# The prompt's attention gates as tanh inside the attention: ScalarE and VectorE in place of sigmoids and Pool's products in the first sample

## The chip, the cores and the metric

The kernel runs on one core of one Trainium2 chip. The metric is device time in microseconds of one launch of the whole kernel; lower is better. All arithmetic is float32.

## The reference, cut to what matters

One decoder layer with two branches. A prompt of 512 tokens and 8 samples of 8 tokens each share one input projection. The attention branch of 16 heads (8 pairs of heads, 64 values each) is multiplied by a SiLU gate of the projected column block `z_a`:

```python
o_a = _prompt_attention(q, keys, vals) * jax.nn.silu(z_a)            # prompt: 512 tokens
o_a_s = _sample_attention(q_s, kv_s, ...) * jax.nn.silu(z_a_s)       # samples: 8 x 8 tokens, 4096 past keys each
# silu(z) = z * sigmoid(z) = 0.5 * z * (1 + tanh(z / 2))
```

The rest of the layer (a low-rank query and key path, an RWKV-7 branch, a gated merge, an output projection) is not touched by the change.

## The kernel before, in words

Each engine has a program of its own; stages follow each other without a barrier, and only semaphores order the engines. The stages are `front` (projection of the latent columns, queries, keys, values), `prompt` (the prompt's attention), `absorb` (a short bridge that folds the key up-projection into the samples' queries), `sample` (8 samples of 4096 keys, each in 8 groups of 512 keys), `rwkv` and `merge`.

`prompt` runs over 8 pairs of heads and, in a pair, over 8 units u (4 blocks of 128 queries, 2 heads), 64 units in all. Unit w of a pair sees (w//2 + 1) x 128 keys. Written out by hand, the order is this:
- TensorE, at step u: scores of unit u+2 (`score`, L727); a few of the 128 matmuls that make the gate columns of `hT` (`gates`, L739), 16 halves e of 288 columns with 8 matmuls each, into two PSUM banks `psZ`; the values of the last two units (`values`, L758) when u is even; at the first step of a pair the spread of the former pair's inverse sums (L771); the transposes of unit u (L748). `values` and `transposes` wait for the copies of the units before (`tr_sb`).
- VectorE, at step u: `top(u)`, the mask, the row maximum and its product (L809, L811, L813). At w = 0, 1, 2 of the next pair also the inverse sums (L819, L823) and `output` (L828, L830): psB is copied to `oaT` and multiplied by the values in `psO`.
- ScalarE, at step u: the exponentials of unit u+2 (L855), which wait for `top(u+2)`, then the copy of unit u's transposes to `pT` (L862), which `values` and the next transposes wait for, then the finished gate half e from `psZ` to `zraw` (`gates_to_sbuf`, L866; the semaphore `z_sb` frees the bank).

So at w = 2 of a pair, VectorE does `top(u)`, then `output` of the former pair, then `top(u+1)`; ScalarE's exponentials of u+1 wait for that, and its copy to `pT` stands behind them.

After the prompt VectorE copies the key weights (L962) and the queries (L967), TensorE makes the absorbed queries (L905), and these go through DRAM to the samples.

`sample` begins with group 0 of sample 0. Per group TensorE makes scores (L1141, L1145) and turns the former group's (L1152); ScalarE copies scores out of PSUM (L1235); VectorE transposes the latents of the group after next (L1285), weights the turned scores (L1321) and keeps a running maximum (L1325, both inputs in SBUF). In sample 0 nothing is yet to be multiplied with the latents, so a group is short. In its first seven groups ScalarE also computes the sigmoid of `zraw`, one pair at a time (`gate_sigmoid`, L912), into the spare tile `sgz`, and GpSimd (Pool) multiplies: `zraw` by the sigmoid (L917), a copy of the sample columns to `zas` (L920), `oaT` by the gate (L921). When all 8 pairs are done (`gated`), the queue of SyncE stores `oaT` to DRAM, and VectorE may weight the first group of sample 1. Much later `gate_samples` (L1387) multiplies the samples' attention by `zas`.

Of the kernel before, what the change touches and what calls it, by code (L numbers as in the profile page):

```python
# [15 lines left out]
KT = D // P  # L16
# [606 lines left out]
def prompt(nc, I, M):  # L623

    with ExitStack() as ctx:
# [11 lines left out]
        M.sgz = pT[:, :, :].rearrange("p a t -> p (a t)")[:, 4 * SEQ - 2 * USED:4 * SEQ].rearrange("p (a t) -> p a t", a=2)  # L637
# [9 lines left out]
        scores, maxed, exped, tr, tr_sb, pv, z_mm, z_sb, inv, inv_tr, inv_sb, spread, o_sb = (  # L647
            sem(n) for n in ("scores", "maxed", "exped", "tr", "tr_sb", "pv", "z_mm", "z_sb", "inv", "inv_tr", "inv_sb", "spread", "o_sb"))
# [4 lines left out]
        M.exped, M.tr_sb, M.zraw_sb, M.pv, M.o_sb = exped, tr_sb, z_sb, pv, o_sb  # L653
# [145 lines left out]
        @block.vector  # L799
        def _(dve):  # L800
            v = nc.vector
            dve.drain()
            dve.wait_ge(fixed_in, 32)

            def top(u):
                hp, qb, nk, c = u // NU, u % NU // 2, cols(u), u % 8
                h = 2 * hp + u % 2
                dve.wait_ge(scores, u + 1)
                v.tensor_tensor(psS[u % 3][:, qb * P:nk], psS[u % 3][:, qb * P:nk], tri[:, :], ALU.add)  # L809
                dve.drain()  # L810
                v.tensor_reduce(mx[:, c:c + 1], psS[u % 3][:, 0:nk], AX.X, ALU.max)  # L811
                dve.drain()
                v.scalar_tensor_tensor(nmx[:, c:c + 1], mx[:, c:c + 1], -1.0, M.qs[:, qb, h:h + 1], ALU.mult, ALU.mult).then_inc(maxed, 1)  # L813

            def inverses(hp):
                dve.wait_ge(exped, NU * (hp + 1))
                if hp > 0:
                    dve.wait_ge(inv_tr, hp)
                v.reciprocal(ri[:, :], rs[:, hp % 2, :]).then_inc(inv, 1)  # L819

            def inverses_to_sbuf(hp):
                dve.wait_ge(inv_tr, hp + 1)
                v.tensor_copy(riT[:, :], psB[0:8, 0:P]).then_inc(inv_sb, 1)  # L823

            def output(hp):
                dve.wait_ge(spread, hp + 1)
                dve.wait_ge(pv, PB * (hp + 1))
                v.tensor_copy(M.oaT[:, hp, 0:SEQ], psB[:, :])  # L828
                dve.drain()
                v.tensor_tensor(M.oaT[:, hp, 0:SEQ], psO[:, :], M.oaT[:, hp, 0:SEQ], ALU.mult).then_inc(o_sb, 1)  # L830

            for u in range(ALL + 3):
                if u < ALL:
                    top(u)
                hp, w = u // NU, u % NU
                if hp > 0:
                    if w == 0:
                        inverses(hp - 1)
                    if w == 1:
                        inverses_to_sbuf(hp - 1)  # L840
                    if w == 2:
                        output(hp - 1)

        @block.scalar
        def _(act):
# [18 lines left out]
            def gates_to_sbuf(e):  # L864
                act.wait_ge(z_mm, e + 1)
                nc.scalar.copy(M.zraw[:, e // 2, e % 2 * HT:(e % 2 + 1) * HT], psZ[e % 2][:, 0:HT]).then_inc(z_sb, 1)  # L866
# [6 lines left out]
            gates_to_sbuf(0)  # L873
            gates_to_sbuf(1)
            for u in range(ALL):
# [3 lines left out]
                for e in range(begun[u] // KT, begun[u + 1] // KT):  # L879
                    gates_to_sbuf(e)  # L880
            for e in range(begun[ALL] // KT, 2 * NP):
                gates_to_sbuf(e)

def absorb(nc, I, M):

    with ExitStack() as ctx:
# [3 lines left out]
        qgT, sg = M.spare[:, 0:NP * SB].rearrange("p (h t) -> p h t", t=SB), M.sgz  # L891
        bank = [ctx.enter_context(nc.psum_tensor(f"ab_bank{i}", [P, 512], F32)) for i in range(8)]
        half_bank, product_banks = (bank[7], bank[5]), ((bank[2], bank[3]), (bank[4], bank[6]))
        tr, tr_sb, mm, ev, act_sb, sigmoids, silus, gated = (sem(n) for n in ("tr", "tr_sb", "mm", "ev", "act_sb", "sigmoids", "silus", "gated"))
# [14 lines left out]
        def gate_sigmoid(act, hp):  # L909
            if hp >= 2:  # L910
                act.wait_ge(silus, hp - 1)
            nc.scalar.activation(sg[:, hp % 2, :], M.zraw[:, hp, :], ACT.Sigmoid).then_inc(sigmoids, 1)  # L912

        def gate(pool, hp):
            v = nc.gpsimd
            pool.wait_ge(sigmoids, hp + 1)
            v.tensor_tensor(M.zraw[:, hp, :], M.zraw[:, hp, :], sg[:, hp % 2, :], ALU.mult).then_inc(silus, 1)  # L917
            pool.wait_ge(M.o_sb, hp + 1)
            pool.drain()
            v.tensor_copy(M.zas[:, hp, :], M.zraw[:, hp, SEQ:USED])  # L920
            v.tensor_tensor(M.oaT[:, hp, 0:SEQ], M.oaT[:, hp, 0:SEQ], M.zraw[:, hp, 0:SEQ], ALU.mult).then_inc(gated, 1)  # L921

        M.absorb_products, M.gate_sigmoid, M.gate_prompt = products, gate_sigmoid, gate
        M.absorb_tr, M.uk_sb, M.absorb_ev, M.gated = tr, uk_sb, ev, gated

# [83 lines left out]
def sample(nc, I, M):  # L1009

    with ExitStack() as ctx:
# [46 lines left out]
        def _(pool):  # L1058
            for hp in range(NP):
                M.gate_prompt(pool, hp)  # L1060
# [167 lines left out]
        def _(act):  # L1228
# [30 lines left out]
            M.gate_sigmoid(act, 0)  # L1259
            M.gate_sigmoid(act, 1)  # L1260
            for i in range(ALL):
                n, g = i // G, i % G
                scores_to_sbuf(i)
                if n == 0 and g > 0 and g + 1 < NP:
                    M.gate_sigmoid(act, g + 1)
# [10 lines left out]
        def _(dve):  # L1276
# [1931 lines left out]
```

## Time and profile before

| | |
|---|---|
| median of 3 runs | 1582.36 us (1582.04 to 1584.71) |
| the profiled execution | 1585.03 us, of which the span from first to last instruction is 1583.2 us |
| prompt's attention, first scores that are waited for to last output | about 186 to 341 us |
| first sample | about 357 to 386 us |
| mean granted TensorE clock | 0.996 |
| TensorE busy, share of the span | 1522.3 us, 96% |
| VectorE, ScalarE, Pool busy | 822.8, 548.6 and 248.8 us |

A row of the timeline has the start and the duration in us, the engine, the line, the operation, output and inputs with their shapes, how many instructions were merged into the row, and in square brackets the idle time of the engine ahead of it and what ended it. PE is TensorE's matmul, PEld its weight load, DVE VectorE, ACT ScalarE, POOL GpSimd. The ends of matmuls are modelled. A matmul of float32 stands in the rows as two instructions.

### The profile page before, as it was taken

The page shows a single profiled execution, that of the slowest core. Times are in us where ns is not written, and L with a number is a line of the kernel's source. Part 1 is how long each engine was busy: PE and PEld are TensorE (multiplying, and loading weights), DVE is VectorE, ACT ScalarE, POOL GpSimd, SP SyncE. Part 2 cuts the span into 40 slices and gives each one's busy share as a digit, 9 for nine tenths or more (in the row PEclk, how much of TensorE's full clock was granted, in tenths as well). Part 3 has the DMA queues.
Part 4 walks back from the last instruction along what each step waited for, and adds up shares of the span by engine and source line. Part 5 has one row for each costly group of instructions (what it writes and reads, how often), then busy time and mean ns, then how long its engine had stood idle before and what let it go on. Part 6 is the DMA issues. An engine that isn't in the chain of part 4 may idle for free.

```text
span 1583.2 us, 40939 instructions
## 1 busy us (share of the span) xinstructions
PE 1522.3 (96%) x16954; PEld 1113.1 (70%) x16954; DVE 822.8 (52%) x1664; ACT 548.6 (35%) x1339; POOL 248.8 (16%) x303
## 2 busy tenths in 40 slices
PE   6999999988999999998999999999999999999998
PEld 4455566657888888776777767677767677777753
DVE  3153445457877777555656565656666522113422
ACT  3056444432222222244353535353535232210000
POOL 0000130235111111110000000000000045446200
PEclk9999999999999999999999999999999999999999
DMA  9713687723455565420112112111111125342302
GB/s 332 275 53 107 204 222 273 197 73 111 126 146 147 144 152 148 112 54 19 35 41 47 50 35 52 30 50 31 49 29 49 33 51 180 80 159 81 113 10 76
DMA packets 192100, 165.30 MB, mean 104 GB/s; under 512 B 38586, under 2 KB 170938, under 8 KB 190892
## 3 DMA queue, kind: packets, MB, share of 16 engines
q1 hardware_dynamic: 182636, 127.13, 28.5%
q0 software_dynamic: 8352, 32.52, 6.7%
q8 instruction: 134, 2.20, 0.6%
q10 hardware_dynamic: 928, 3.05, 0.6%
q14 instruction: 50, 0.41, 0.1%
HBM read 136.97 MB, written 25.69 MB: 103 GB/s over the span
## 4 chain that ended last, share of the span: by engine, by line
PE 65%; DVE 6%; ACT 5%; DVEq 2%; issue 2%; DMA 0%; SPq 0%; POOL 0%; ACTq 0%
PE me_bank L2902 12%; PE rw_bank L1715 10%; PE sa_psOs L1182 7%; PE sa_psS L1145 7%; PE me_bank L2922 3%; PE rw_bank L1754 2%; PE sa_psT L1152 2%; DVE rw_gram L2479 2%; PE sa_psS L1141 2%; PE rw_bank L1816 2%; PE rw_bank L1835 1%; PE rw_bank L1727 1%; PE rw_bank L1740 1%; PE rw_bank L1967 1%; PE rw_bank L1887 1%
## 5 line engine op out<-in xcount | busy, mean ns | idle before, releaser
L1715 PE MATMUL rw_bank<-hT,big 128*128 128x288 f32 x672 | 183.6, 418 | 0.0
L1715 PEld LDWEIGHTS rw_bank<-hT,big 128*128 128x128 f32 x672 | 122.4, 190 | 32.4 <-issue 1.2
L1235 ACT COPY kpe<-sa_psS 128x512 f32<-128x512 f32 x64 | 37.5, 586 | 211.4 <-PE sa_psS L1145 211.4
L1513 POOL COPY shc<-prep 128x3 f32<-128x3 f32 x8 | 1.5, 190 | 473.0 <-ACT rw_xs L2181 473.0
L1740 PE MATMUL rw_bank<-hT,big 128*128 128x288 f32 x256 | 73.5, 421 | 0.0
L739 PE MATMUL pr_psZ<-hT,qlT 128*128 128x288 f32 x256 | 73.1, 406 | 0.1
L1321 DVE TENSOR_TENSOR sa_ST<-sa_psT,kinvp 128x512 f32<-128x512 f32 x64 | 43.8, 685 | 50.2 <-PE sa_psT L1152 47.2
L2961 ACT COPY big<-me_bank 128x288 f32<-128x288 f32 x42 | 16.8, 399 | 144.8 <-PE me_bank L2902 144.8
L855 ACT ACTIVATE pr_pb<-pr_psS,pr_nmx,qs 128x128 f32<-128x128 f32 (+3 forms) x64 | 39.5, 618 | 77.3 <-PE pr_psT L748 46.3
L1145 PE MATMUL sa_psS<-sa_cT_blocks,qg 32*128 32x128 f32 x2048 | 64.6, 274 | 0.0
L1145 PE MATMUL sa_psS<-sa_cT_blocks,qlT 32*128 32x128 f32 x2048 | 63.0, 270 | 0.0
L2499 DVE COPY_PREDICATED rw_X<-lev,rw_bank 128x128 f32<-128x128 int32 (+1 forms) x80 | 20.9, 261 | 79.6 <-PE rw_bank L1835 79.6
L1182 PE MATMUL sa_psOs<-big,sa_ST 128*128 128x257 f32 x256 | 61.1, 381 | 1.2 <-ACT sa_ol_raw L1251 1.2
L1182 PE MATMUL sa_psOs<-pages,sa_ST 128*128 128x257 f32 x256 | 61.0, 381 | 1.2 <-ACT sa_ol_raw L1251 1.2
L1145 PEld LDWEIGHTS sa_psS<-sa_cT_blocks,qg 32*128 32x128 f32 x2048 | 61.9, 191 | 0.0
L739 PEld LDWEIGHTS pr_psZ<-hT,qlT 128*128 128x128 f32 x256 | 46.9, 189 | 20.7 <-issue 9.0
L1145 PEld LDWEIGHTS sa_psS<-sa_cT_blocks,qlT 32*128 32x128 f32 x2048 | 60.3, 187 | 0.0
L1740 PEld LDWEIGHTS rw_bank<-hT,big 128*128 128x128 f32 x256 | 44.9, 189 | 20.1 <-issue 11.5
L994 POOL DMA_DIRECT2D pages<-in_cache_kv x68 | 37.6, 553 | 126.8 <-issue 126.8
L994 POOL DMA_DIRECT2D big<-in_cache_kv x68 | 37.6, 554 | 118.4 <-issue 118.4
L2902 PE MATMUL me_bank<-prep,me_arena 128*128 128x288 f32 x208 | 53.4, 406 | 0.0
L1182 PEld LDWEIGHTS sa_psOs<-pages,sa_ST 128*128 128x128 f32 x256 | 46.5, 190 | 8.2 <-ACT sa_ol_raw L1251 1.9
(547 smaller groups left out, 3346.4 us busy)
## 6 DMA issues: line engine op xcount, KB each, us to landing
big<-in_w_in SPq DMA_DIRECT2D x44, 512.0 KB, 4.0
big<-in_cache_kv POOLq DMA_DIRECT2D x68, 128.0 KB, 3.2
pages<-in_cache_kv POOLq DMA_DIRECT2D x68, 128.0 KB, 2.8
fr_wada<-in_w_ada SPq DMA_DIRECT2D x8, 1024.0 KB, 11.4
big<-in_cache_kv SPq DMA_DIRECT2D x60, 128.0 KB, 2.9
pages<-in_cache_kv SPq DMA_DIRECT2D x60, 128.0 KB, 3.0
qk_scratch<-oaT SPq DMA_DIRECT2D x32, 192.0 KB, 2.5
fr_wada<-in_w_ada SPq DMA_DIRECT2D x2, 2048.0 KB, 10.4
```

The lines of the kernel that those rows point to most:

```text
L739: last = nc.tensor.matmul(psZ[h][:, 0:HT], M.wz[hp % 2][:, k, :], M.hT[:, k, h * HT:(h + 1) * HT], start=(k == 0), stop=(k == KT - 1))
L855: nc.scalar.activation(pb[:, u % 2, 0:cols(u)], psS[u % 3][:, 0:cols(u)], ACT.Exp, bias=nmx[:, c:c + 1], scale=M.qs[:, qb, h:h + 1], accum ...
L994: e.dma_start(M.pages[s % 2][q * QP:(q + 1) * QP, g, :, 0:KL], src).then_inc(landed, 16)
L1141: nc.tensor.matmul(psS[:, b, 0:ROW], M.qpT[rows, n, :, :].rearrange("p h t -> p (h t)"), kT[rows, g, :], start=True, stop=False)
L1145: done = nc.tensor.matmul(psS[:, b, 0:ROW], q4[n % 2][rows, a, :], cT[rows, g % 2, a, :], start=False, stop=(a == NCB - 1))
L1182: done = nc.tensor.matmul(psO[:, 0:C1], STs[s % 2][:, GP * g + c, :], M.pages[s % 2][:, g, c, :], start=(g == 0 and c == 0), stop=False)
L1235: nc.scalar.copy(S[:, i % 2, :].rearrange("q (c p j) -> q p c j", c=GP, p=GP), got).then_inc(copied, 1)
L1321: v.tensor_tensor(group, psT[i % 2][:, :].rearrange("p (a h t) -> p a h t", h=H, t=TD), bc(ki, TD, 3), ALU.mult).then_inc(weighted, 1)
L1715: last = mm(bank[h][:, 0:HT], w[:, ORDER[q], k, :], M.hT[:, k, (F0, F1)[h]], start=(k == 0), stop=(k == KT - 1))
L1740: last = mm(bank[h][:, 0:HT], w[:, 3, k, :], M.hT[:, k, (F0, F1)[h]], start=(k == 0), stop=(k == KT - 1))
L2902: last = nc.tensor.matmul(into[:, 0:HT], st[:, k, :], mv[:, k, :], start=(k == 0 and n in (1, 2, 7)), stop=(k == KT // 2 - 1), skip_group_ ...
L2922: last = nc.tensor.matmul(out_bank[o][:, :], mT[k][:, b * P:(b + 1) * P], wo[k][:, n * 512:(n + 1) * 512], start=(k == 0), stop=(k == KT - 1))
```

## The change

ScalarE reads each finished gate half from PSUM through `Tanh` with scale 0.5, in place of the plain copy. VectorE then computes (tanh + 1) * z from `zraw` and the PSUM bank, which is twice the SiLU; only then is the bank free. `output` of a pair gets a third operation: `oaT` = (gate * 0.5) * `oaT`. The sample columns go straight to `zas`, and `gate_samples` multiplies by 0.5 as well. The sigmoids on ScalarE and everything of Pool's in the first sample are removed, with the spare tile and VectorE's wait for `gated` at sample 1.

VectorE takes the halves three steps after TensorE finished them, behind `top(u)`; halves 0 and 1 behind `top(1)`. Worked out from the tables `in_pair`, half e is taken at u = 6, 10, 14, 19, 24, 28, 33, 37, 42, 46, 51, 56, 62, 66 for e = 2 to 15, which is w = 6, 2, 6, 3, 0, 4, 1, 5, 2, 6, 3, 0, 6, 2.

```diff
+                dve.drain()
+                v.scalar_tensor_tensor(M.oaT[:, hp, 0:SEQ], M.zraw[:, hp, 0:SEQ], 0.5, M.oaT[:, hp, 0:SEQ], ALU.mult, ALU.mult).then_inc(gated, 1)
+            def twice_silu(e):
+                hp = e // 2
+                dve.wait_ge(z_tanh, e + 1)
+                if e % 2 == 0:
+                    half = M.zraw[:, hp, 0:HT]
+                    v.scalar_tensor_tensor(half, half, 1.0, psZ[0][:, 0:HT], ALU.add, ALU.mult).then_inc(z_sb, 1)
+                else:
+                    half = M.zraw[:, hp, HT:SEQ]
+                    v.scalar_tensor_tensor(half, half, 1.0, psZ[1][:, 0:SEQ - HT], ALU.add, ALU.mult)
+                    v.scalar_tensor_tensor(M.zas[:, hp, :], M.zraw[:, hp, SEQ:USED], 1.0, psZ[1][:, SEQ - HT:HT], ALU.add, ALU.mult).then_inc(z_sb, 1)
             for u in range(ALL + 3):
                 if u < ALL:
                     top(u)
+                if u == 1:
+                    twice_silu(0)
+                    twice_silu(1)
+                if u >= 3:
+                    for e in range(begun[u - 3] // KT, begun[u - 2] // KT if u - 2 < ALL else 2 * NP):
+                        twice_silu(e)
...
-                nc.scalar.copy(M.zraw[:, e // 2, e % 2 * HT:(e % 2 + 1) * HT], psZ[e % 2][:, 0:HT]).then_inc(z_sb, 1)
+                nc.scalar.activation(M.zraw[:, e // 2, e % 2 * HT:(e % 2 + 1) * HT], psZ[e % 2][:, 0:HT], ACT.Tanh, scale=0.5).then_inc(z_tanh, 1)
...
-        def gate_sigmoid(act, hp):
-            if hp >= 2:
-                act.wait_ge(silus, hp - 1)
-            nc.scalar.activation(sg[:, hp % 2, :], M.zraw[:, hp, :], ACT.Sigmoid).then_inc(sigmoids, 1)
-        def gate(pool, hp):
-            v = nc.gpsimd
-            pool.wait_ge(sigmoids, hp + 1)
-            v.tensor_tensor(M.zraw[:, hp, :], M.zraw[:, hp, :], sg[:, hp % 2, :], ALU.mult).then_inc(silus, 1)
-            pool.wait_ge(M.o_sb, hp + 1)
-            pool.drain()
-            v.tensor_copy(M.zas[:, hp, :], M.zraw[:, hp, SEQ:USED])
-            v.tensor_tensor(M.oaT[:, hp, 0:SEQ], M.oaT[:, hp, 0:SEQ], M.zraw[:, hp, 0:SEQ], ALU.mult).then_inc(gated, 1)
...
-            for hp in range(NP):
-                M.gate_prompt(pool, hp)
...
-                        dve.wait_ge(M.gated, NP)
...
-                v.tensor_tensor(M.zas[:, :, :], o, M.zas[:, :, :], ALU.mult).then_inc(gated, 1)
+                v.scalar_tensor_tensor(M.zas[:, :, :], M.zas[:, :, :], 0.5, o, ALU.mult, ALU.mult).then_inc(gated, 1)
```

## Rows read from the trace of the kernel before

**Rows 1.** Windows, 150 us of prompt, 24 of first sample: busy us (instructions).

```profile
195.00:345.00 150.00, 143.25 (x937) 99.56 (x935) 72.67 (x214) 71.65 (x199) 41.24 (x72) 1.00 0.71 206
362.00:386.00 24.00, 20.57 (x545) 18.17 (x549) 19.94 (x20) 7.60 (x13) 18.46 (x18) 1.00 0.11 30
```

**Rows 2.** Waits, 180 to 345 us: us in total, times, longest.

```profile
PE pr_psO L758 <- ACT pr_pT L862: 5.3, 9, 0.7
```

**Rows 3.** Timeline at `output` of the first pair (w = 2 of the second).

```profile
208.58 0.69 DVE L828 COPY oaT<-pr_psB 128x512 f32<-128x512 f32 x1 [2.05 <-PE pr_psB L771]
...
209.35 0.69 DVE L830 TENSOR_TENSOR oaT<-pr_psO,oaT 128x512 f32<-128x512 f32 x1
...
210.80 1.14 PE L739 MATMUL pr_psZ<-hT,qlT 128*128 128x288 f32 x4
...
211.01 0.56 ACT L855 ACTIVATE pr_pb<-pr_psS,pr_nmx,qs 128x256 f32<-128x256 f32 x1 [1.30 <-DVE pr_nmx L813]
...
211.57 0.25 ACT L862 COPY pr_pT<-pr_psT 128x128 f32<-128x128 f32 x1
...
211.87 0.44 PE L758 MATMUL pr_psO<-pr_pT,pr_vh 128*64 128x128 f32 x4
```

**Rows 4.** Timeline in the last pair, behind `output` of the seventh.

```profile
325.03 0.44 PE L758 MATMUL pr_psO<-pr_pT,pr_vh 128*64 128x128 f32 x4 [0.58 <-ACT pr_pT L862]
```

**Rows 5.** Timeline at the start of the prompt's attention.

```profile
186.71 0.30 DVE L809 TENSOR_TENSOR pr_psS<-pr_psS,pr_tri 128x128 f32<-128x128 f32 x1
...
188.10 0.69 ACT L866 COPY pr_zraw<-pr_psZ 128x288 f32<-128x288 f32 x2
...
188.67 0.59 ACT L855 ACTIVATE pr_pb<-pr_psS,pr_nmx,qs 128x256 f32<-128x256 f32 x1
...
189.23 0.28 ACT L862 COPY pr_pT<-pr_psT 128x128 f32<-128x128 f32 x1
...
190.17 0.27 PE L748 MATMUL pr_psT<-ident_sb,pr_pb 128*128 128x128 f32 x1
```

**Rows 6.** Timeline behind the last `output`.

```profile
341.09 1.22 DVE L962 COPY pr_wuk<-ab_bank 128x512 f32<-128x512 f32 x2
...
343.49 3.79 PE L905 MATMUL ab_bank<-pr_pb,pr_wuk 64*128 64x64 f32 x64 [0.38 <-DVE pr_pb L967]
```

**Rows 7.** Groups of VectorE by shape: busy us, mean ns, idle before.

```profile
L3011 DVE TENSOR_TENSOR me_arena<-me_bank,big 128x288 f32<-128x288 f32 x16 | 7.3, 458 | 68.8 <-ACT big L2961 35.2 <-PE me_bank L2902 33.6
...
L2531 DVE TENSOR_TENSOR rw_ZRm<-rw_bank,rw_ZR 128x64 f32<-128x64 f32 x8 | 1.7, 214 | 0.0
```

**Rows 8.** Timeline of the first sample, groups 2 to 4, and group 8.

```profile
365.13 0.50 PE L1141 MATMUL sa_psS<-sa_kpeT_blocks,qpT 32*128 32x128 f32 x8 [0.20 <-ACT kpe L1235]
...
368.21 0.50 PE L1141 MATMUL sa_psS<-sa_kpeT_blocks,qpT 32*128 32x128 f32 x8 [0.20 <-ACT kpe L1235]
...
368.73 1.40 POOL L917 TENSOR_TENSOR pr_zraw<-pr_zraw,pr_pT 128x576 f32<-128x576 f32 x1
368.83 1.85 DVE L1325 TENSOR_TENSOR sa_top<-sa_ST 128x512 f32<-128x512 f32 x1
...
371.89 0.50 PE L1141 MATMUL sa_psS<-sa_kpeT_blocks,qpT 32*128 32x128 f32 x8 [0.80 <-DVE sa_cT_blocks L1285]
...
385.57 0.50 PE L1141 MATMUL sa_psS<-sa_kpeT_blocks,qpT 32*128 32x128 f32 x8 [0.21 <-ACT kpe L1235]
```

**Rows 9.** Line L1325 in the whole run: duration in ns, least, median, most.

```profile
L1325 DVE TENSOR_TENSOR sa_top<-sa_top,sa_ST x48: 691/692/1705, 372.5 to 648.5; 128x512 f32<-128x512 f32 x48
```

**Rows 10.** Timeline at the first exponentials of the samples.

```profile
395.61 1.28 ACT L1242 ACT_TABLE_LOAD   x1
...
396.40 1.28 DVE L1344 TENSOR_TENSOR sa_ST<-sa_ST,sa_topB 128x512 f32<-128x512 f32 x2
...
397.12 1.23 ACT L1245 ACTIVATE sa_ST<-sa_ST 128x512 f32<-128x512 f32 x2
```

**Rows 11.** ScalarE's timeline at the tanh behind the samples' last exponentials.

```profile
670.40 0.68 ACT L2320 ACTIVATE big<-big 64x576 f32<-64x576 f32 x1 [3.32 <-DVE big L2606]
```

More of the change, by code:

```diff
@@ L646, in prompt @@
         fixed_in, heads_in = sem("fixed_in"), [sem("heads_in0"), sem("heads_in1")]
-        scores, maxed, exped, tr, tr_sb, pv, z_mm, z_sb, inv, inv_tr, inv_sb, spread, o_sb = (
-            sem(n) for n in ("scores", "maxed", "exped", "tr", "tr_sb", "pv", "z_mm", "z_sb", "inv", "inv_tr", "inv_sb", "spread", "o_sb"))
+        scores, maxed, exped, tr, tr_sb, pv, z_mm, z_tanh, z_sb, inv, inv_tr, inv_sb, spread, o_sb, gated = (
+            sem(n) for n in ("scores", "maxed", "exped", "tr", "tr_sb", "pv", "z_mm", "z_tanh", "z_sb", "inv", "inv_tr", "inv_sb", "spread", "o_sb", "gated"))
         w_v = I["w_in"].rearrange("(k p) n -> p k n", p=P)
@@ L652, in prompt @@
         block = M.block
-        M.exped, M.tr_sb, M.zraw_sb, M.pv, M.o_sb = exped, tr_sb, z_sb, pv, o_sb
+        M.exped, M.tr_sb, M.zraw_sb, M.pv, M.o_sb, M.gated = exped, tr_sb, z_sb, pv, o_sb, gated
         cols = lambda u: (u % NU // 2 + 1) * P
@@ L872, in _ @@
             exponentials(1)
-            gates_to_sbuf(0)
-            gates_to_sbuf(1)
+            gates_tanh(0)
+            gates_tanh(1)
             for u in range(ALL):
@@ L879, in _ @@
                 for e in range(begun[u] // KT, begun[u + 1] // KT):
-                    gates_to_sbuf(e)
+                    gates_tanh(e)
             for e in range(begun[ALL] // KT, 2 * NP):
-                gates_to_sbuf(e)
+                gates_tanh(e)
 def absorb(nc, I, M):
@@ L890, in absorb @@
         ukT = M.wuk[:, :, :]
-        qgT, sg = M.spare[:, 0:NP * SB].rearrange("p (h t) -> p h t", t=SB), M.sgz
+        qgT = M.spare[:, 0:NP * SB].rearrange("p (h t) -> p h t", t=SB)
         bank = [ctx.enter_context(nc.psum_tensor(f"ab_bank{i}", [P, 512], F32)) for i in range(8)]
         half_bank, product_banks = (bank[7], bank[5]), ((bank[2], bank[3]), (bank[4], bank[6]))
-        tr, tr_sb, mm, ev, act_sb, sigmoids, silus, gated = (sem(n) for n in ("tr", "tr_sb", "mm", "ev", "act_sb", "sigmoids", "silus", "gated"))
+        tr, tr_sb, mm, ev, act_sb = (sem(n) for n in ("tr", "tr_sb", "mm", "ev", "act_sb"))
         uk_sb = sem("uk_sb")
@@ L907, in products @@
             last.then_inc(mm, 1)
-        def gate_sigmoid(act, hp):
-            if hp >= 2:
-                act.wait_ge(silus, hp - 1)
-            nc.scalar.activation(sg[:, hp % 2, :], M.zraw[:, hp, :], ACT.Sigmoid).then_inc(sigmoids, 1)
-        def gate(pool, hp):
-            v = nc.gpsimd
-            pool.wait_ge(sigmoids, hp + 1)
-            v.tensor_tensor(M.zraw[:, hp, :], M.zraw[:, hp, :], sg[:, hp % 2, :], ALU.mult).then_inc(silus, 1)
-            pool.wait_ge(M.o_sb, hp + 1)
-            pool.drain()
-            v.tensor_copy(M.zas[:, hp, :], M.zraw[:, hp, SEQ:USED])
-            v.tensor_tensor(M.oaT[:, hp, 0:SEQ], M.oaT[:, hp, 0:SEQ], M.zraw[:, hp, 0:SEQ], ALU.mult).then_inc(gated, 1)
-        M.absorb_products, M.gate_sigmoid, M.gate_prompt = products, gate_sigmoid, gate
-        M.absorb_tr, M.uk_sb, M.absorb_ev, M.gated = tr, uk_sb, ev, gated
+        M.absorb_products, M.absorb_tr, M.uk_sb, M.absorb_ev = products, tr, uk_sb, ev
         @block.tensor
```

7 lines of the change are left out of this document (1 added, 6 removed).

## The prediction

> **What bounds the kernel now.** I read the windows first, because the change moves work between two stages. In 150 us of the prompt [rows 1] TensorE has matmuls for 143.25 us, VectorE and ScalarE for 72.67 and 71.65: the reader is to see a stage that TensorE bounds, with two helpers half idle. That alone would say that new work of VectorE there is free. The waits [rows 2] say the same: TensorE waited for the copies to `pT` for 5.3 us in all. But in a stage where three engines take turns a half idle engine can still be in line at one place. So I read the timeline next, at the places where VectorE gets new work, and followed each step to the matmul behind it. The first sample, the second window of [rows 1], is another case: VectorE is busy for 19.94 of 24 us, Pool for 18.46, TensorE for 20.57, so there TensorE waits 3.4 us in 24.
>
> **ScalarE's tanh for the copy.** 16 reads of 128x288 out of PSUM at 0.35 to 0.4 us (two for 0.69) [rows 5] become 16 activations of the same shape. The nearest activation, with its function read from a table, took 0.59 us for 256 columns with two pointer operands and an accumulator, the copy is shorter; an immediate scale should cost next to nothing, at most 0.1 us each. Hidden: ScalarE is idle half of the time. 
>
> **VectorE's halves.** An operation on 288 columns with one input in PSUM took 0.46 us, on 64 columns 0.21 [rows 7]; for 224 columns I put 0.21 + 160/224 x 0.24 = 0.39. An even half costs 0.46, an odd one 0.39 + 0.21 = 0.60, eight of each 8.5 us. Halves 2 to 15 stand behind `top(u)`, three steps late, when the tanh should be done; the cover is VectorE's wait for the next scores or, at w = 2, its wait of 2.05 us for the spread [rows 3]. I take 0 for these 14. If that cover were gone, all 14 would cost 7 x 0.46 + 7 x 0.60 = 7.4 us. The two at w = 3 (halves 5 and 12) have the thinnest cover, since `output` has just made VectorE late; 0 to 0.5 us each.
>
> **The start.** Halves 0 and 1 are not three steps late. `top(2)` began at 186.71, and now stands behind both halves, which wait for tanh. Those come where the copies are, at 188.10 to 188.79, the first done at about 188.5 [rows 5]. Half 0 then ends at 188.97, half 1 at 189.36 and 189.6. `top(2)` starts at 189.6 and takes about 1.0 (from the end of L830, 210.04, to the exponentials at 211.01 it is 0.97 for the same width [rows 3]), so the exponentials of unit 2 start at 190.6 and not at 188.67. Behind them on ScalarE is the copy of unit 0, which ended at 189.51 and now ends at 191.4, and on TensorE the transposes of unit 1, which came at 190.17 and would come at 191.45: **1.3 us** lost. Bounds: 0.5 (TensorE has more queued than the modelled ends say) and 2.0 (the whole delay of the exponentials).
>
> **The third operation of `output`.** It is 128x512, and L828 to L830, with a drain between, is 209.35 - 208.58 = 0.77 us [rows 3]; the new one adds the same again. What stands behind it? `top(11)`, then ScalarE's exponentials of unit 11, which waited for VectorE (idle 1.30), then on ScalarE the copy of unit 9 (ends 211.82), then the values of TensorE at 211.87. TensorE's gate matmuls ahead of these end at 210.80 + 1.14 = 211.94 [rows 3]. So the chain from VectorE is already in line with TensorE there, with less than 0.1 us to spare. The same rows come behind the outputs of pairs 1 to 6, of which the first is shown. So the copy comes 0.77 late, and TensorE stands for 0.7: 6 x 0.7 = **4.2 us**. In the last pair TensorE has fewer gate matmuls and already stood 0.58 us at this place [rows 4]: **0.77**. Bounds of these seven: from 0.4 each (2.8) to 0.9 each (6.3). Nothing gives it back later, since TensorE's own work then sets the pace.
>
> **Behind the last `output`** VectorE goes on without a gap: L830 to 341.03, the key weights at 341.09, then copies that TensorE waits for until 343.49 [rows 6]. The new operation pushes that whole chain: **0.77 us**. It goes on through the queries to DRAM and back, on which the samples wait, so it isn't hidden. SyncE's queue is not held: its store of `oaT` waits for `gated`, which now comes before it reaches that place, so the 2 MB leave some 20 us earlier, behind the loads of sample 1's queries.
>
> **What the first sample gains.** Pool's products ran together with VectorE's L1325: from 368.83 it took 1.85 us beside L917 [rows 8], where its median in the run is 692 ns [rows 9]. The latents behind it came late and TensorE waited for them (0.80). From group 3 to group 8 it is 385.57 - 368.21 = 17.36 us for five groups, 3.47 each; undisturbed, 368.21 - 365.13 = 3.08 [rows 8]. Five times 3.08 is 15.40, a gain of 1.96; VectorE's transposes of the next keys fall in one of them, so I take **1.9 us**, with bounds of 1.2 and 2.3. The Trainium skill ("SBUF — State Buffer", Who interferes with whom) has the rule: a VectorE instruction with two SBUF inputs and a GpSimd one that reads SBUF exclude each other; the trace agrees with 1.85 against 0.69. By the same rule the new product of `output`, with both inputs in SBUF, could stand behind Pool in the prompt; but there Pool only issues transfers.
>
> **The two table loads.** The sigmoids' load goes, and so does the exponentials' at 395.61, 1.28 us. The exponentials of the scores started at 397.12; VectorE's centring, which they also need, ran from 396.40 for two groups in 1.28, the first done at about 397.05 [rows 10]. So the load is covered: 0, at the most 1.3. The 0.5 in `gate_samples` is a second scalar of one instruction: 0. Pool has nothing else to do in that time: 0.
>
> **The sum.** 1.3 + 4.2 + 0.77 + 0.77 - 1.9 = +5.1 us. The profiled execution took 1585.03 (span 1583.2), so it would be 1590.1; it was itself 2.7 above the median of the runs, to which I add: 1582.36 + 5.1 = 1587.5.
>
> **The rivals.**
> - *The third product is hidden too.* The ends of matmuls are modelled; if TensorE has 0.8 us more queued than the rows say when it reaches the values at w = 2, six pairs cost nothing, and 1.3 + 0.77 + 0.77 - 1.9 = +0.9: 1583.3. For it: only 5.3 us of waits in all [rows 2]. Against it: VectorE's chain ends within 0.1 us of TensorE's [rows 3], and in the last pair TensorE stood [rows 4]. It decides from 0.3 us more slack per pair, which takes 1.8 off the forecast. 0.2.
> - *The first sample pays for all, faster.* The table load at 395.61 is on the path (1.28), Pool's hold is worth its upper bound (2.3), and the prompt hides what it can: 0.9 + 1.9 - 2.3 - 1.28 = -0.8, still no gain above 0.2%. To be faster by that, the start and the last product must be hidden as well: 1582.36 - 2.3 - 1.28 = 1578.8. 0.04.
> - *VectorE's halves are not covered.* A half waits for its tanh in front of the next `top`; from 0.5 us per half on it shows. With the 7.4 us above in full, 1594.9; with a third of it, 1590. 0.14.
> - *Tanh is loaded from another set.* Then each of 16 tanh brings two loads of 1.28 us, as the one of [rows 10], 41 us on ScalarE, of which its idle time of some 1.3 us [rows 3] covers half: some 20 us, 1607. Against it [rows 11]. 0.02.
>
> **How the numbers follow.** The forecast has 0.6. What a measurement of this kernel can tell from no change is about 0.2%, 3.2 us, so slower means above 1585.5 and faster below 1579.2. Slower: 0.6 less a tenth for its lower bounds (0.5 + 2.8 + 0.77 + 0.77 - 2.3 = +2.5), plus 0.14 and 0.02, some 0.70; the hidden product lies within 0.2%; faster 0.04. The range goes from 1582.5, under the first rival, to 1591.0, the forecast with upper bounds for start and products (+0.7 and +1.4) and 1.4 us of uncovered halves; outside it lie the rest of the third rival and the last, and the second.
>
> **What the profile after would show.** L748 of unit 1 some 1.3 us later against the first scores; at w = 2 of each pair a TensorE wait for L862 of about 0.7 us, so that the waits [rows 2] grow from 5.3 to about 11 and each pair gets 0.7 us longer; L905 0.8 later behind the last `output`; in the first sample L1325 at 0.69 throughout and groups of 3.08 us; no load at L1242; no wait of TensorE for `z_sb`. I am wrong if the pairs take the same time as before, or if VectorE waits for tanh in the middle of the prompt.

## The result and the profile after

The changed kernel takes 1593.03 us (median of 4 runs, 1592.73 to 1593.34), the kernel before 1583.17 us in the same comparison (4 runs, 1582.04 to 1584.71): a ratio of 1.0059 [1.0044, 1.0074], 9.9 us slower. The forecast was 1587.5 with a range up to 1591.0, so the direction was right and the size was not.

The profiled execution after took 1593.19 us, its span is 1591.5; before, 1585.03 and 1583.2. Of 9.9 us between the medians the two traces therefore show 8.3.

The waits of TensorE, 180 to 345 us, answer to [rows 2]. They doubled, as forecast (11 us).

```profile
PE pr_psO L757 <- ACT pr_pT L880: 11.1, 15, 1.4
```

The timeline of the changed kernel at the first `output` answers to [rows 3]. L831 is the new operation, and TensorE's values, which came at 211.87 without a wait, now come at 215.25 after 0.73 us of waiting for ScalarE's copy, behind exponentials that waited for VectorE:

```profile
211.17 0.69 DVE L827 COPY oaT<-pr_psB 128x512 f32<-128x512 f32 x1 [1.61 <-PE pr_psB L770]
211.94 0.69 DVE L829 TENSOR_TENSOR oaT<-pr_psO,oaT 128x512 f32<-128x512 f32 x1
212.72 0.69 DVE L831 SCALAR_TENSOR_TENSOR oaT<-pr_zraw,oaT 128x512 f32<-128x512 f32 x1
213.39 1.13 PE L738 MATMUL pr_psZ<-hT,qlT 128*128 128x288 f32 x4
214.39 0.56 ACT L873 ACTIVATE pr_pb<-pr_psS,pr_nmx,qs 128x256 f32<-128x256 f32 x1 [2.09 <-DVE pr_nmx L812]
214.94 0.25 ACT L880 COPY pr_pT<-pr_psT 128x128 f32<-128x128 f32 x1
215.25 0.44 PE L757 MATMUL pr_psO<-pr_pT,pr_vh 128*64 128x128 f32 x4 [0.73 <-ACT pr_pT L880]
```

In the last pair the same place waits 1.38 us; before it was 0.58 [rows 4].

```profile
329.74 0.69 DVE L827 COPY oaT<-pr_psB 128x512 f32<-128x512 f32 x1 [1.78 <-PE pr_psB L770]
333.82 0.44 PE L757 MATMUL pr_psO<-pr_pT,pr_vh 128*64 128x128 f32 x4 [1.38 <-ACT pr_pT L880]
```

The start of the prompt's attention answers to [rows 5]. VectorE stood 1.91 us for the first tanh; the transposes of unit 1 came at 191.82 and not at 190.17. The gate products waited 0.56 us for the bank that half 0 frees, which the forecast had ruled out (no wait of TensorE for `z_sb`):

```profile
186.63 0.60 PE L726 MATMUL pr_psS<-pr_kh,pr_qh 96*128 96x256 f32 x2
188.50 0.70 ACT L884 ACTIVATE pr_zraw<-pr_psZ 128x288 f32<-128x288 f32 x2
188.94 0.46 DVE L838 SCALAR_TENSOR_TENSOR pr_zraw<-pr_zraw,pr_psZ 128x288 f32<-128x288 f32 x1 [1.91 <-ACT pr_zraw L884]
189.54 2.48 PE L738 MATMUL pr_psZ<-hT,qlT 128*128 128x288 f32 x6 [0.56 <-DVE pr_zraw L838]
191.82 0.42 PE L747 MATMUL pr_psT<-ident_sb,pr_pb 128*128 128x128 f32 x1
```

Behind the last `output`, for [rows 6], TensorE stands 1.13 us and not 0.38. The next row is what the forecast did not have: the 64 absorbed products take 6.12 us in place of 3.79.

```profile
353.03 6.12 PE L923 MATMUL ab_bank<-pr_pb,pr_wuk 64*128 64x64 f32 x64 [1.13 <-DVE pr_pb L970]
```

Windows of the changed kernel show why: the column behind POOL is TensorE's granted clock (1.00 is 2.4 GHz, 0.50 is 1.2). About 1 us after that pause it is at half, and it had also fallen at the start, where before it stayed at 1.00.

```profile
190.00:192.00 2.00, 2.00 (x7) 1.19 (x6) 1.41 (x6) 0.81 (x3) 1.74 (x3) 0.57 0.95 234
192.00:194.00 2.00, 2.00 (x7) 1.24 (x5) 0.37 (x2) 0.81 (x3) 1.14 (x3) 0.57 0.99 418
...
352.00:354.00 2.00, 0.97 (x18) 1.00 (x19) 1.97 (x4) 0.00 (x0) 0.00 (x0) 1.00 0.04 8
354.00:356.00 2.00, 2.00 (x25) 2.00 (x23) 0.23 (x1) 0.00 (x0) 0.00 (x0) 0.53 0.00 0
356.00:358.00 2.00, 2.00 (x22) 2.00 (x22) 1.06 (x2) 0.00 (x0) 0.00 (x0) 0.50 0.04 8
```

In the first sample, for [rows 8], TensorE's timeline (starts of L1142) has groups of 3.07 to 3.08 us (372.19 to 375.26, 378.34, 381.41), and L1321, line L1325 of before [rows 9], takes 694 ns at most. The gain is there. But one group takes 5.67 us (381.41 to 387.08), with a pause in the middle of its scores that no semaphore explains:

```profile
369.11 0.50 PE L1142 MATMUL sa_psS<-sa_kpeT_blocks,qpT 32*128 32x128 f32 x8 [1.32 <-DMA qg<-q_lat_scratch]
372.19 0.50 PE L1142 MATMUL sa_psS<-sa_kpeT_blocks,qpT 32*128 32x128 f32 x8 [0.79 <-ACT kpe L1236]
...
381.41 0.50 PE L1142 MATMUL sa_psS<-sa_kpeT_blocks,qpT 32*128 32x128 f32 x8 [0.20 <-ACT kpe L1236]
385.80 0.50 PE L1146 MATMUL sa_psS<-sa_cT_blocks,qg 32*128 32x128 f32 x6 [2.15 <-issue]
387.08 0.50 PE L1142 MATMUL sa_psS<-sa_kpeT_blocks,qpT 32*128 32x128 f32 x8 [0.20 <-ACT kpe L1236]
...
396.36 0.50 PE L1142 MATMUL sa_psS<-sa_kpeT_blocks,qpT 32*128 32x128 f32 x8 [0.21 <-ACT kpe L1236]
```

The DMA queues of the changed kernel from 376 to 383 us: the store of `oaT` fills them, and q8, whose packets the profile calls instructions, has none at all. Its next one, recorded at 383.4, comes 9.2 us after the one before, where the kernel before has 4.7 to 6.7 us between two of them in the first sample.

```profile
q1 hardware_dynamic: 1537, 2.25, 86.6%
issues: line engine op xcount, KB each, median us to landing
oa_scratch<-oaT SPq DMA_DIRECT2D x1, 2048.0 KB, 8.8
```

**The account of the two traces.** After less before, from one row to the answering one; "own" is what the stretch itself adds, and the sums in brackets are what has added up by its end. Unmarked rows are in [rows 3], [rows 6] and [rows 8] or in the fences; the seventh `output` of before began at 321.74, its first scores of the samples at 357.35 and the second at 362.05, group 8 at 385.57.

| stretch | own us | forecast |
|---|---|---|
| up to the scores of unit 2, ahead of the change (186.07 to 186.63) | +0.56 | 0 |
| to the transposes of unit 1 (+1.65 there) | +1.09 | 1.3 |
| to the first `output` (+2.59), granted clock 0.57 | +0.94 | 0 |
| six pairs, to the seventh `output` (+8.00) | +5.41 | 4.2 |
| to the absorbed products (+9.54) | +1.54 | 0.77 + 0.77 |
| to the first scores of the samples (+11.76) | +2.22 | 0 |
| first group of the samples, at half clock before only (4.70 to 3.08) | -1.62 | 0 |
| seven groups, Pool's products gone | -1.94 | -1.9 |
| the group with the pause, 5.67 less 3.08 | +2.59 | 0 |
| the rest, to the product with the samples' gates (708.4 to 719.5) | +0.3 | 0 |
| from there to the end of the span | -2.8 | 0 |

The last row is a stretch at half clock that the profiled execution of before had and that of after did not, in the layer behind the attention. Windows of before, then of the changed kernel at the same work:

```profile
720.00:725.00 5.00, 4.51 (x155) 2.96 (x155) 1.90 (x8) 3.31 (x10) 0.00 (x0) 0.79 0.01 3
725.00:730.00 5.00, 4.43 (x83) 3.09 (x82) 1.76 (x6) 2.73 (x8) 0.00 (x0) 0.53 0.07 16
```

```profile
730.00:735.00 5.00, 3.89 (x148) 2.56 (x149) 2.48 (x9) 3.32 (x13) 0.00 (x0) 1.00 0.02 5
735.00:740.00 5.00, 3.66 (x117) 2.79 (x105) 2.20 (x7) 3.84 (x9) 0.00 (x0) 1.00 0.06 16
```

### The profile page after: what moved, and what is told of

Same layout as the page of the kernel before. It is cut to its first block, busy times and chain, and to the rows that moved or that the text cites. A ratio compares the mean times of both kernels' runs of the same rounds, so it can differ in the third digit from the quotient of the medians.

```text
span 1591.5 us, 40937 instructions
## 1 busy us (share of the span) xinstructions
PE 1525.0 (96%) x16954; PEld 1114.7 (70%) x16954; DVE 830.6 (52%) x1696; ACT 541.0 (34%) x1329; POOL 223.6 (14%) x279
## 4 chain that ended last, share of the span: by engine, by line
PE 65%; DVE 6%; ACT 5%; DVEq 2%; issue 2%; DMA 0%; SPq 0%; POOL 0%; ACTq 0%
PE me_bank L2898 12%; PE rw_bank L1711 9%; PE sa_psS L1146 7%; PE sa_psOs L1183 7%; PE me_bank L2918 3%; PE rw_bank L1750 2%; PE sa_psT L1153 2%; DVE rw_gram L2475 2%; PE sa_psS L1142 2%; PE rw_bank L1812 1%; PE rw_bank L1831 1%; PE rw_bank L1723 1%; PE rw_bank L1736 1%; PE rw_bank L1963 1%; PE rw_bank L1883 1%
```

## The experiments

Three sets on three chips; the kernel before took 1583.70, 1584.02 and 1583.66 us beside them (20 or 21 runs each). Ratios are to it, "changed" is the changed kernel (1593.03 us, beside 1583.17 for the kernel before), so a difference to it in us is good to about 1 us. Where two intervals overlap (changed with a, c, g and h; i with b, e and l), it is the traces that carry the comparison. Diffs are against the changed kernel where nothing else is said.

**a: the store of `oaT` later.**

```diff
             sp.wait_ge(M.gated, NP)
+            sp.wait_ge(turned, 9)
             sp.dma_start(M.oa_dram[:, :, 0:SEQ]
```

> The changed kernel with one wait more in SyncE's queue: the 2 MB store of oaT leaves only when the scores of group 6 of the first sample have been turned, about where it left in the kernel before. In the changed kernel TensorE stood for 2.15 us in the middle of the scores of group 4 (383.66 to 385.80), waiting for nothing that the profile shows, while the store, issued at 376.75, was landing (8.8 us). Theory A: TensorE's next instructions come in by DMA and stood behind the store's packets. Then the gap is gone here, the first sample ends 2.2 to 2.5 us earlier, and the whole is about 2.3 us faster than the changed kernel (1590.7). Rival: the gap belongs to TensorE's code as it now lies in time, whatever the store does; then it stays at the same group with 2.15 us, and the time is 1593.

Measured: 1590.19 us (5 runs), 1.0044 [1.0030, 1.0058], 2.8 below changed. The pause is gone, the groups where it was take 3.08 (378.70 to 381.78):

```profile
381.78 0.50 PE L1143 MATMUL sa_psS<-sa_kpeT_blocks,qpT 32*128 32x128 f32 x8 [0.20 <-ACT kpe L1237]
```

The two traces part by more than the store. At the first scores of the samples a's stands at 366.40, 2.7 us ahead of changed: at the start its clock stayed at 1.00, though the code up to there is the same, and the products took 4.70 us and not 6.12, as less of them fell to half clock. Up to the product with the samples' gates (714.25) 2.6 us more are gained, which are the store's. Behind the attention a has two stretches at half clock that changed has not, at 722 and 732 us. A cleaner pair is b and i below.

**b: `output` in two operations.** Gates, halved, times the spread reciprocals straight from PSUM, then the output; no third product.

```diff
-                v.tensor_copy(M.oaT[:, hp, 0:SEQ], psB[:, :])
+                dve.drain()
+                v.scalar_tensor_tensor(M.oaT[:, hp, 0:SEQ], M.zraw[:, hp, 0:SEQ], 0.5, psB[:, :], ALU.mult, ALU.mult)
                 dve.drain()
                 v.tensor_tensor(M.oaT[:, hp, 0:SEQ], psO[:, :], M.oaT[:, hp, 0:SEQ], ALU.mult).then_inc(o_sb, 1)
-                dve.drain()
-                v.scalar_tensor_tensor(M.oaT[:, hp, 0:SEQ], M.zraw[:, hp, 0:SEQ], 0.5, M.oaT[:, hp, 0:SEQ], ALU.mult, ALU.mult).then_inc(gated, 1)
```

> The changed kernel with output of two operations again: (gate * 0.5) * psB into oaT, then times psO. The third product of 128x512 is gone at all eight places, nothing else. Theory: it is in line with TensorE at each, 0.79 us for each pair by the distance of the outputs (211.17 to 329.74 against 208.58 to 321.74) and 0.75 behind the last: 6.3 us faster than the changed kernel, 1586.7, and the waits for pT go back to about 5.3 us. Rival, that most of the pairs' loss comes from the gate halves beside it: then less than 3 us comes back.

Measured: 1583.16 us (10 runs), 0.9999 [0.9989, 1.0008]: 9.9 below changed, all that the change cost, and 3.5 us more than was expected. TensorE's wait in the pairs is back at [rows 2]'s, and the products are at full clock behind a pause of 0.41:

```profile
PE pr_psO L757 <- ACT pr_pT L879: 5.3, 9, 0.7
```

```profile
346.18 3.79 PE L922 MATMUL ab_bank<-pr_pb,pr_wuk 64*128 64x64 f32 x64 [0.41 <-DVE pr_pb L969]
```

From the first to the seventh `output` b takes 113.6 us (210.78 to 324.40), changed 118.57 and before 113.16. So of the 9.9 us the pairs up to there are 5.0, the last one and what is behind it 1.5, and the rest is not in the third product's own rows: it also brings the pause behind which the clock falls (products of 6.12 us in place of 3.79). b still has the start's wait and a pause of 2.01 us in the first sample. Its clock fell later, behind a wait of 1.38 us at 351 us that the kernel before has too, at 348.66, and there without a fall.

**c: the first two halves one unit later each.**

```diff
-                if u == 1:
-                    twice_silu(0)
-                    twice_silu(1)
+                if u in (2, 3):
+                    twice_silu(u - 2)
```

> The changed kernel with gate half 0 taken behind top(2) and half 1 behind top(3), in place of both behind top(1). Theory: top(2) is no longer held by the tanh, so the stall of 1.2 us at the transposes of unit 1 is gone but for some 0.4 us in which the gate matmuls wait for the bank; and TensorE's clock, which fell to 0.57 in 190 to 194 us behind that stall and cost 0.9 us more, stays at 1.00 as in the kernel before. 1.7 us faster: 1591.3. Rival: the fall of the clock there has to do with the time since the last one and not with the stall; then only 0.8 us comes back and the window at 190 still shows about 0.57.

Measured: 1594.99 us (4 runs), 1.0070 [1.0052, 1.0089], 2.0 above changed: a miss. VectorE no longer delays unit 2, but the gate products still waited 0.56 us for the bank that half 0 frees, TensorE's clock fell at the start all the same, and a further stretch at half clock lay behind the attention. At the product with the samples' gates (718.32) its trace is still 1.2 us ahead of changed, so what it loses lies behind that. To move the halves does not mend the start.

**d: the kernel before without any gate of the prompt.** The store of `oaT` waits for the last `output` alone, and the samples' gates are zero. Against the kernel before:

```diff
-            for hp in range(NP):
-                M.gate_prompt(pool, hp)
...
-            M.gate_sigmoid(act, 0)
-            M.gate_sigmoid(act, 1)
...
-                        dve.wait_ge(M.gated, NP)
```

> The kernel before with all gates of the prompt left out: no sigmoids, none of Pool's products, oaT stays without its gate and the samples' gate is set to zero; the store of oaT waits for the last output alone and so leaves as early as in the changed kernel. What this gains is what freeing the first sample is worth by itself. By my sum 1.9 us (L1325 back at 0.69, groups of 3.08 us): 1581. If theory A of the store holds, TensorE stands some 2 us in the first sample here too, and the gain is about nothing: 1583.

Measured: 1580.88 us (10 runs), 0.9982 [0.9972, 0.9991]. So all sigmoids, Pool's products and their contention were worth 2.8 us to the kernel before. That is the ceiling of what the change could take away, and it set out to pay for it with VectorE's time on the path.

**h: TensorE's pause ahead of the absorbed products filled.**

```diff
+            pe.wait_ge(act_sb, 2)
+            for _ in range(12):
+                nc.tensor.transpose(bank[2][:, 0:P], M.ident[:, :], M.ident[:, :])
```

> The changed kernel, with TensorE's 1.13 us without work ahead of the absorbed products (353.0 us) filled by twelve transposes of the unit matrix into a bank that is free, about 0.87 us at the 72 ns each of the sixteen transposes just before. They compute nothing that is used. Theory (the fall of the granted clock to 0.50 from 354 to about 364 us follows that pause): the granted clock stays at 1.00 until at least the last absorbed product, the 64 products take about 3.8 us in place of 6.1 and the whole 1590.7 +- 0.7 us, that is 2.3 us under the changed kernel. Rival (the clock falls for what comes before the pause, or at a time of its own): the products still take over 6 us at a granted clock of 0.50, and the time is that of the changed kernel, 1593 +- 0.7 us. Second rival (the pause does it, and another pause brings the same fall a few us later): the products take 3.8 us, but a stretch at 0.50 falls upon the four loads of qlT or the first scores, and the time is within 1 us of the changed kernel's.

Measured: 1591.03 us (4 runs), 1.0050 [1.0035, 1.0065], 2.0 below changed. The products are at full clock, at 3.79 us, with nothing before them but work that computes nothing:

```profile
351.48 1.53 PE L951 MATMUL ab_bank<-ident_sb 128*128 128x128 f32 x12
352.94 3.79 PE L923 MATMUL ab_bank<-pr_pb,pr_wuk 64*128 64x64 f32 x64
```

The fall only moved, as the second rival said. A wait of 1.39 us at 358.12 left the clock at 1.00; the fall came with the pause of 3.35 us ahead of the first scores, and lasted over two groups, 5.0 us each:

```profile
364.00:366.00 2.00, 0.00 (x0) 0.00 (x0) 0.89 (x2) 0.00 (x0) 0.00 (x0) 1.00 0.70 204
366.00:368.00 2.00, 1.17 (x20) 1.20 (x24) 0.00 (x0) 0.00 (x0) 0.00 (x0) 0.50 0.89 218
```

By the third group h was 1.6 us behind changed; it had no pause beside the store, though, and by the sixth it was 1.0 ahead. Here the fall went with the pause; where the time is paid depends on what is next.

**f: the third product twice.**

```diff
+                v.scalar_tensor_tensor(M.oaT[:, hp, 0:SEQ], M.zraw[:, hp, 0:SEQ], 0.5, M.oaT[:, hp, 0:SEQ], ALU.mult, ALU.mult)
+                dve.drain()
```

> The changed kernel with its third operation of an output (the product with the gates) done twice, so the output's values are gated twice and scaled by a half once more. Theory (the output's third operation stands on the path in all eight pairs, 0.79 us in each of seven and 0.75 us after the last): one more costs the same again, 7 x 0.79 + 0.75 = 6.3 us, that is 1599.3 +- 1 us, with the milestones of the pairs moving on by 0.79 us each and TensorE's wait ahead of the absorbed products going from 1.13 to 1.9 us. The clock may add up to 3 us where a longer pause brings another stretch at 0.50. Rival (the third product is mostly hidden and the 9.9 us come from the clock and the start): below 1596 us, with pairs that move on by under 0.4 us each.

Measured: 1600.30 us (4 runs), 1.0102 [1.0087, 1.0118], 7.3 above changed. From the first to the seventh `output` it is 334.21 - 211.37 = 122.84 us, changed has 118.57: 0.76 to 0.78 more in five of the six intervals and 0.42 in one, 0.71 on average. The wait in front of the products is 0.77 longer, and TensorE's waits in the pairs grew by 5.0 us, where the first product had brought 5.8:

```profile
PE pr_psO L757 <- ACT pr_pT L882: 16.1, 15, 2.1
```

```profile
360.32 7.09 PE L925 MATMUL ab_bank<-pr_pb,pr_wuk 64*128 64x64 f32 x64 [1.90 <-DVE pr_pb L972]
```

**g: no halves.** The tanh alone gates the output, and the samples' gates are zero.

> The changed kernel without the products of the tanh's results with the gates (VectorE's halves, 16 times 0.46 us or 0.38 and 0.21 us): the output is multiplied by the tanh alone and the samples' gates are zero. The third product of each output stays. Theory (the halves are hidden in the pairs and cost 1.2 us at the start and about 0.3 us at the last): 1591.5 +- 0.8 us, with the pairs moving on by 0.79 us each as before. Rival (the halves are the cause of the pairs' 0.79 us, not the third product): 1587 us or below, with pairs that move on by under 0.3 us.

Measured: 1591.34 us (5 runs), 1.0045 [1.0030, 1.0060], 1.7 below changed. From the first to the seventh `output` it takes 118.07 us (208.35 to 326.42), changed 118.57, before 113.16: the halves are 0.50 of the 5.41 us, the third product (with the tanh) 4.91: 0.78 or 0.79 in five of the intervals and 0.98 in one. The transposes of unit 1 come 3.96 us behind the scores of unit 2 and not 5.19, so the halves are the start's:

```profile
185.97 0.60 PE L727 MATMUL pr_psS<-pr_kh,pr_qh 96*128 96x256 f32 x2
...
189.93 0.27 PE L748 MATMUL pr_psT<-ident_sb,pr_pb 128*128 128x128 f32 x1
```

**i: b with the late store of a.**

> The changed kernel with the output in two operations (the gates, halved, by the spread reciprocals first, then by the output) and with the store of the prompt's output held back until the ninth transposed group of the first sample. Theory (the store's 2 MB beside the first sample's instructions stopped TensorE's queue for 2.0 us with the fused output as for 2.2 us in the changed kernel): holding it back takes these 2.0 us away; 1583.2 of the fused kernel less 2.0 to 2.8 gives 1580.8 +- 0.8 us, 0.15% below the kernel before. Rival (the stall is given back later, in the sample whose own loads the later store meets): 1583.2 +- 0.7 us, no different from the fused kernel, with a later stretch of TensorE that is longer by about 2 us.

Measured: 1581.03 us (11 runs), 0.9985 [0.9976, 0.9994], 2.1 below b. In b one group took 5.34 us, here all of that stretch take 3.08. The 2.26 us are kept: the product with the samples' gates stands at 709.69 in b and 705.37 here, 4.32 apart, and the first scores were 2.06 apart (359.92 and 357.86).

```profile
376.28 0.31 PEld L1145 LDWEIGHTS sa_psS<-sa_cT_blocks,qg 32*128 32x128 f32 x6 [2.01 <-issue]
```

That row is b's; its store was under way from 366.9, and in the same 6.6 us (366.9 to 373.5) its instruction queue has no packet, that of i two:

```profile
q8 instruction: 2, 0.03, 1.9%
```

**e: i with the halves of c.**

> As the one before (fused output, late store), with the first two gate halves taken up at the third and fourth unit in place of the second. Theory (the 1.2 us of the start come from VectorE waiting for the tanh in front of the second unit's reciprocals, and the later halves cost the start 0.4 to 0.7 us in place of 1.2 to 1.6): 0.5 to 0.8 us below its neighbour, 1580.2 +- 0.8 us. Rival (the later halves keep the gates' banks so much longer that the gate products wait for them, as the later halves alone brought 1595.0 and not 1592): the same as its neighbour or up to 2 us above, about 1582 us, with TensorE waiting over 0.5 us for a half ahead of the gate products.

Measured: 1582.44 us (11 runs), 0.9988 [0.9979, 0.9998], 1.4 above i. It is not the gain that was expected, and the rival's sign is there: the gate products waited 0.56 us, and the granted clock was 0.50 from 190 to 192 us.

**d with the late store.**

> The kernel before without any gates of the prompt (the prompt's output isn't gated and the samples' gates are zero), with its store held back until the ninth transposed group of the first sample. With the early store it took 1580.9 us, with no stop of TensorE in the first sample though the store ran there. Theory (the store delays a transfer of instructions only where one falls due while it runs; there it began as the store was issued, at 363 us): with the late store no stop either, 1580.7 +- 0.7 us. Rival (the early store costs the first sample some 2 us by the traffic alone, beside the instructions): 1578.8 +- 0.7 us.

Measured: 1581.09 us (10 runs), 0.9986 [0.9977, 0.9996], the same as d. A 2 MB store in the first sample costs nothing by its traffic.

**l: the first tanh into ScalarE's idle time.** Against i:

```diff
+            act.wait_ge(M.front_stored, 80)
+            gates_tanh(0)
             act.wait_ge(M.front_done, 1)
             act.wait_ge(M.cnew_done, 1)
-            act.wait_ge(M.front_stored, 80)
             exponentials(0)
             exponentials(1)
-            gates_tanh(0)
             gates_tanh(1)
...
-                if u == 1:
-                    twice_silu(0)
-                    twice_silu(1)
+                if u in (1, 2):
+                    twice_silu(u - 1)
```

> The fused output and the late store, and at the start the first gate half's tanh ahead of the first unit's exponentials, behind the wait for the front's stores alone; the first half is taken up by VectorE at the second unit, the second at the third. Theory (at the start ScalarE stands 7.6 us and then loads its table, 1.28 us, on the path behind the first maxima, and VectorE waits 1.9 us for two tanhs): the table load and the first tanh (0.35 us) now lie in that idle time, the exponentials of the first unit begin 1.28 us earlier and the transposes of the second unit 1.5 to 2.5 us earlier; 1581.0 less that is 1579.0 +- 1 us, 0.3% below the kernel before. Rival (behind the first exponentials another thing is late, TensorE's gate products or the page transfers, and the prompt's attention is paced by them): the start gives back under 0.5 us and the time is 1581 +- 0.7 us. Second rival (the front's stores end after the first maxima): no move of the table load, the same time.

Measured: 1578.98 us (10 runs), 0.9972 [0.9962, 0.9981], 2.1 below i and 4.7 below the kernel before. The two medians are 2.1 apart, but the two profiled executions stand level at the samples' gates (705.49, i 705.37): l has its first `output` 1.4 us earlier and lost that in the first group, 4.58 us at half clock in place of 3.08. The table load, which in the other kernels stands on the path behind the first maxima, ran at 181.65, and VectorE takes half 0 without a wait:

```profile
181.65 1.28 ACT L882 ACT_TABLE_LOAD   x1 [3.51 <-PE pr_psZ L738]
182.94 0.41 ACT L882 ACTIVATE pr_zraw<-pr_psZ 128x288 f32<-128x288 f32 x1
185.76 0.46 ACT L871 ACTIVATE pr_pb<-pr_psS,pr_nmx,qs 128x128 f32<-128x128 f32 x1 [2.41 <-DVE pr_nmx L812]
...
186.38 0.45 DVE L837 SCALAR_TENSOR_TENSOR pr_zraw<-pr_zraw,pr_psZ 128x288 f32<-128x288 f32 x1
```

## Why the prediction was wrong in its size

**Right.** *Behind the last `output`* and the last pair: 0.77 + 0.77, measured 1.54. *What the first sample gains*: 1.9, measured 1.94, by the mechanism named. *The start*: 1.3, measured 1.1 in the trace, 1.2 by g, and 1.3 in a and h, whose code is the same up to there and whose clock stayed at 1.00. That TensorE would not wait for `z_sb` was wrong (0.56 us); but in a the transposes behind it still waited 0.52 us for ScalarE's copy, and in h as well, so the path that the prediction named set the time. *VectorE's halves* 2 to 15: hidden but for 0.5 us in all (g); they show in two of the six intervals between outputs, of 20.02 and 20.05 us, where three others take 19.69. *ScalarE's tanh*: 420 ns where the copy had some 0.4, with no load. The load of [rows 10] went and nothing was gained, as forecast. The rival in which the third product is hidden is refuted by b and f, that of uncovered halves by g, that of tanh's table by the trace.

**Wrong, the third operation of `output`, by its size.** It was put at 0.7 us for each of six pairs; the chain was taken to have 0.07 of slack. By g's intervals it cost 0.78 or 0.79 in five of them, the whole operation with no slack, and 0.98 in one: 4.91 over six, which with the halves' 0.50 makes 5.41 in place of 4.2, 1.2 us more. f gives 0.76 to 0.78 in five for one operation more, so the mechanism holds. Why one interval costs g 0.98 is open.

**Wrong, "nothing gives it back later, since TensorE's own work then sets the pace".** The sum moved each operation in time and left TensorE's own durations as they were. But the pause that it computed right ahead of the absorbed products was followed by a fall of the granted clock to 0.50: 2.2 us (the 64 products alone 6.12 less 3.79). All thirteen profiled executions agree at this place:

| TensorE's wait ahead of the 64 products | executions | the products took |
|---|---|---|
| 0.34 to 0.41 us | before, b, d, d with the late store, e, i, l | 3.79 us in all |
| 1.13 us | changed, a, c, g | 6.12, 4.70, 6.43, 6.49 us |
| 1.90 us | f | 7.09 us |
| 1.13 us filled with transposes | h | 3.79 us |

So at this place the pause does it. At the start it is not shown: the 0.94 us of the changed kernel's trace come from a clock of 0.57, behind waits of 1.00 and 0.56 us. The clock fell there in c and e too, but stayed at 1.00 in a, b, f, h and i, with a wait of 0.9 to 1.3 us and the same 0.56. From the scores of unit 2 to the first `output` changed takes 24.54 us, a 23.88 and h 23.89 with the same code, so a fall there costs some 0.65 us in the executions that have it. Nor does a pause's length alone decide elsewhere: the 1.38 us in changed's last pair left the clock at 1.00. What decides is open.

Where the clock had fallen at these products or the few matmuls behind them, it did not fall again at the first scores in six executions of seven (changed, a, b, c, f, i; g is the other); where it had not, it fell there in all six. The kernel before paid 1.62 us for that in its first group. The profile before held the warning: matmuls at half clock behind a wait of 3.33 us at 357 us. The Trainium skill ("TensorE: Matmul & The Clock Gate", What's actually happening) says that the clock depends on how busy the array has been of late. The traces agree in that it fell behind a wait; that the same waits at the start went with and without a fall shows that a wait by itself gives no price.

**Wrong, SyncE's store at nothing.** The prediction saw that the 2 MB leave some 20 us earlier, and costed only what waits in SyncE's queue. The account that fits is that TensorE's instructions come by the same DMA engines: the group with the stop took 2.59 us more in changed, 2.26 in b, 1.7 in c and 2.2 in f, and there is none with the late store (a, i). In those four the packet of q8 came 8.2 to 9.2 us behind the one before, and TensorE went on 2.2 to 2.5 us after it. In g and h the store was as early and the packet as late (7.2 and 8.0 us), but TensorE did not stop: its groups ahead of it ran at half clock, up to 5.0 us each, and so may have used up its instructions later, which is argued and not shown. d shows the other condition: its store ran beside the first sample too, but its transfers of instructions came at 363.4, as the store was issued, and at 369.5, as its traffic ended, and TensorE did not stop. The Trainium skill ("Runtime: NRT & Kernel Launch", Instruction fetch mechanics) calls the cost of crossing from one block of instructions to the next mostly hidden; with a 2 MB store under way it was not in four of these traces.

**Together.** The missed items in the changed kernel's trace are 0.94 (the clock at the start) + 1.2 (the pairs) + 2.2 (the clock behind the pause) + 2.6 (the store) = 6.9 us, against the 1.6 that came back at the first group and 0.3 besides; 5.1 + 6.9 - 1.6 + 0.3 - 0.2 (the start) + 0.6 (ahead of the change) = 11.1, which is what stands at the samples' gates. The remaining -2.8 lies with the execution of before that was profiled, which took 1.9 us more than the median of its runs. Which executions have a half clock stretch behind the attention is open: of the thirteen profiled here only the changed kernel and b had none. For this reason a difference of two whole traces is good to some 3 us here, and no run removes it.

Why c, whose trace differs from changed by little up to the samples, is 2 us slower is not settled beyond that its profiled execution has such a stretch at 735 us.

## What to carry to other kernels

An engine that is busy half of the time, as VectorE was here, can have no free time at the points where it is next in line: follow each new operation to the matmul behind it, and fold a product into an operation that is there anyway (here the spread reciprocals' copy) before adding one. Where a sum makes a new pause of TensorE, put the slower clock of the matmuls behind it into the range (here 0.9 to 3.3 us for 64 products), and where it moves a large transfer, ask whose instructions come meanwhile. An idle engine's table load and first activation belong ahead of the wait that ends its idle time: that, the two-operation output and the later store make the fastest version here, 1578.98 us against 1583.66; without that step the other two (i) had 1581.03 against 1584.02.

## What the runs showed of the hardware

- TensorE's granted clock fell to 0.50 behind a pause of 1.13 us and stayed at 1.00 behind one of 0.41 at the same place; with the 1.13 us filled by transposes it stayed at 1.00 until a pause of 3.35 us. 64 products took from 3.79 to 7.09 us by how much of them fell into such a stretch. At the start of the prompt's attention waits of 0.9 to 1.3 and 0.56 us went with a fall in three executions and without one in five.
- A 2 MB store kept the DMA queues at about 400 GB/s for some 7 us, and in the changed kernel and in b no packet of the instruction queue was recorded in 7.0 and 6.6 us of it; TensorE then stood 2.15 and 1.82 us without a semaphore to wait for (1.28 in c, 1.76 in f, nothing in g and h).
- One VectorE operation of 128x512 with all operands in SBUF or one in PSUM took 0.69 us in either form: as a copy of PSUM, as a product of PSUM with SBUF, and as a product of two SBUF tiles. So a copy out of PSUM could carry a product at no price here.
